# Router logits with the weights stationary in two column halves of the array, in a one-core transformer layer

## The chip, the core and the metric

The kernel runs on one core of a Trainium2 chip. Its engines are TensorE (PE, with its weight loads shown apart as PEld), VectorE (DVE), ScalarE (ACT), GpSimd (POOL) and SyncE (SP), which issues most transfers (SPq is its queue). The metric is the device time of one execution in microseconds (us), less being better; what is compared is the median of several executions.

## What is computed

One layer with 512 tokens and a model width of 1024, all float32: a mixer (gated recurrences), a layer norm, and a mixture of experts with 64 experts of which each token takes 6, beside a shared expert. The change lies in the router at the head of the mixture:

```python
def moe_ffn(h, router_w, router_bias, we_gate, we_up, we_down, ws_gate, ws_up, ws_down):
    xt = h.reshape(B * L, D)                                     # 512 x 1024
    scores = jax.nn.sigmoid((xt @ router_w).astype(jnp.float32)) # 512 x 64
    _, idx = lax.top_k(scores + router_bias, TOP_K)
    s_sel = jnp.take_along_axis(scores, idx, axis=-1)
    wts = s_sel / jnp.sum(s_sel, axis=-1, keepdims=True) * ROUTED_SCALE
    y = routed_experts(xt, idx, wts, we_gate, we_up, we_down) + swiglu(xt, ws_gate, ws_up, ws_down)
```

## The kernel before, in words

The tokens are four tiles of 128 (TT = 4, T = 512); the contraction of 1024 is 8 blocks of 128 (KB = 8); E = 64 experts, P = 128. The first part of the kernel (to about 500 us) is the mixer. `out_and_route` follows, and then `experts`, which works through the expert weights pair by pair from a ring of buffers in on-chip memory, with SP issuing the loads (`load_chunk`, L784) as buffers come free.

Inside `out_and_route` the order of work is written out by hand for each engine; engines meet at semaphores. On PE: `project(2)`, `project(3)` (L170, the output projection of a tile), `turn(t)` (eight transposes of a tile of h1, the normed hidden state, L1033), `logits(t)` (L1039), then `shared_up(0)` (L1046, the shared expert's first product), the counting of the chosen experts (L1083 to L1091), and so on until the tables that say which token goes to which expert's slot. On DVE: `mixed(t)` (L1165 to L1171) and `normed(t)` (L1175 to L1177, whose last step sets `h1_ready`), then the choice of experts, whose first use by PE waits for `chosen_ready` (set by L1207), then the tables; the last of its steps sets `tables_read` (L1280), for which SP waits before it issues further expert weights. On ACT: `root(t)` (L1133, a square root for tile t's norm), `take(t)` (L1137, the copy of a turned tile from PSUM to `h1T`, which sets `h1T_taken`), the sigmoid (L1149). ACT's order is `root(0)`, `root(1)`, `root(2)`, `take(0)`, `take(1)`, `root(3)`, `take(2)`, `take(3)`, sigmoid.

The logits of a tile before the change: the stationary operand is a block of h1T (128 x 128, so 128 columns are loaded), the moving one is the block of the router's weights (128 x 64), and eight products add up in a 64-column strip of bank 0 (R), tokens on partitions. Each float32 product shows as two matmul records and two weight loads in the trace. The column a product writes to in the array follows from where its output starts in PSUM: `gate_up` in `experts` (L1382) writes the two experts of a pair to the two halves of the partitions, with 64-column weights, and `down` (L1423) writes quarters.

Of the kernel before, what the change touches and what calls it, by code (L numbers as in the profile page):

```python
# [18 lines left out]
P = 128  # L19
D = 1024  # L20
KB = D // P
META = 16
T = 512
TA = META + T
TT = T // P
# [12 lines left out]
E = 64  # L38
# [43 lines left out]
ACT = mybir.ActivationFunctionType  # L82
# [29 lines left out]
def program(nc, a, out, stop=9, dbg=None):  # L112
    with ExitStack() as whole:
# [49 lines left out]
        with nc.Block() as block:  # L163
            out_and_route(nc, block, a, sem, sb, banks, pair, mem, top, raw_at, pairs)
            experts(nc, block, a, sem, mem, pairs, out)
# [615 lines left out]
def load_chunk(sp, a, sem, to, name, expert, c):  # L781

    src = a["w_gate_up"][expert, :, c] if c < 2 else a["w_down"][expert]
    return sp.dma_start(to, src).then_inc(sem(name), 16)  # L784


def chunk_at(mem, third, s, c):

    return mem["first"][:, PAIR * c + s] if third == 2 else mem["raw"][:, CHUNKS * (PAIR * third + s) + c]


def raw_here(third, c):

    return f"raw_here_{third}_{c}"
# [109 lines left out]
def out_and_route(nc, block, a, sem, sb, banks, pair, mem, top, raw_at, pairs):  # L904
# [8 lines left out]
    def sb_first(name, shape):  # L913
        at = low[0]
        low[0] += (int(np.prod(shape[1:])) * 4 + 63) // 64 * 64
        assert low[0] <= top[0], name
        return sb(name, shape, at=at)

    h1T = sb_first("h1T", [P, KB, T])
# [3 lines left out]
    rw = sb_first("rw", [P, KB, E])  # L923
# [3 lines left out]
    onehot = sb_first("onehot", [P, ITEMS])  # L927
    count = sb_first("count", [P, EXTRA])
    steps6 = sb_first("steps6", [P, STEPS])
    e_col = sb_first("e_col", [P, 1])  # L930
    tok = sb_first("tok", [P, TT, 2])
    stats = sb_first("stats1", [P, TT, 2, 6])
    mv = sb_first("mv1", [P, TT, 2])
    rs = sb_first("rs1", [P, TT, 2])
# [3 lines left out]
    def sb_late(name, shape):  # L938
        at = late[0]
        late[0] += (int(np.prod(shape[1:])) * 4 + 63) // 64 * 64  # L940
        assert late[0] <= raw_at + RING * CHUNK_W * 4, name
        return sb(name, shape, at=at)
# [3 lines left out]
    sc = sb_late("scores", [P, TT, E])  # L946
# [23 lines left out]
    R, PO, SM = banks[0], banks[1], banks[7]  # L970
# [8 lines left out]
    @block.sync  # L979
    def _(sp):  # L980
        sp.dma_start(g1[:], a["norm_rows"][2:3].broadcast_to([P, D])).then_inc(sem("ln1_here"), 16)
        sp.dma_start(b1[:], a["norm_rows"][3:4].broadcast_to([P, D])).then_inc(sem("ln1_here"), 16)
        for t, n in ((rw, "router_w"), (rbias, "router_bias"), (before, "before"), (before2, "before2"),
                     (count, "count"), (steps6, "steps6"), (e_col, "e_col"), (iota, "iota"),
                     (onehot, "onehot"), (tok, "tok")):
            src = a[n].broadcast_to([P, E]) if n == "router_bias" else a[n]
            sp.dma_start(t[:], src).then_inc(sem("route_here"), 16)
        sp.dma_start(ws_gu[:], a["ws_gate_up"]).then_inc(sem("shared_here"), 16)
        sp.dma_start(ws_dn[:], a["ws_down"]).then_inc(sem("shared_here"), 16)
        sp.dma_start(pairs.tok_row[:], a["tok_row"]).then_inc(sem("tok_row_here"), 16)  # L990

        def bring(third, u, c):
            load_chunk(sp, a, sem, chunk_at(mem, third, u, c), raw_here(third, c), PAIR * third + u, c)

        def ring(slot):
            bring(slot // (CHUNKS * PAIR), slot // CHUNKS % PAIR, slot % CHUNKS)

        for slot in range(NORM_CHUNK):
            if slot not in (MERGED_CHUNK, MERGED_CHUNK + 1):
                ring(slot)  # L1000
        for t in range(TT):
            sp.wait_ge(sem("h1_ready"), t + 1)
            sp.dma_start(h1_rows[t * P:(t + 1) * P], acc[:, t]).then_inc(sem("h1_stored"), 16)

        sp.wait_ge(sem("mix_done"), TT)
        for slot in (MERGED_CHUNK, MERGED_CHUNK + 1, NORM_CHUNK):
            ring(slot)
        sp.wait_ge(sem("tables_read"), 1)
        for slot in range(NORM_CHUNK + 1, RING):
            ring(slot)  # L1010
        sp.wait_ge(sem("shared_up_done"), 4)
        for c in range(2):
            for u in range(PAIR):
                bring(2, u, c)
        bring(2, 1, 2)
        sp.wait_ge(sem("shared_done"), TT)
        bring(2, 0, 2)

    @block.tensor
    def _(pe):  # L1020
# [7 lines left out]
        def turn(t):  # L1028
            pe.wait_ge(sem("h1_ready"), t + 1)
            if t >= 2:  # L1030
                pe.wait_ge(sem("h1T_taken"), t - 1)
            for k in range(KB):
                last = pe.transpose(pair[2 + t % 2][:, k * P:(k + 1) * P], acc[:, t, k::KB], ident[:])  # L1033
            last.then_inc(sem("h1T_done"), 1)

        def logits(t):
            pe.wait_ge(sem("h1T_taken"), t + 1)
            for k in range(KB):
                last = pe.matmul(R[:, t * E:(t + 1) * E], h1T[:, k, t * P:(t + 1) * P], rw[:, k],  # L1039
                                 start=(k == 0), stop=(k == KB - 1))  # L1040
            return last

        def shared_up(i, ks=range(KB)):
            m = gate_first[i]
# [21 lines left out]
            turn(t)  # L1066
        project(3)
        turn(2)
        pe.wait_ge(sem("route_here"), 16 * 10)

        pe.wait_ge(sem("mix_taken"), 3)
        for t in range(TT - 1):
            logits(t)
        turn(TT - 1)
        logits(TT - 1).then_inc(sem("logits_done"), 1)

        pe.wait_ge(sem("shared_here"), 32)
        pe.wait_ge(sem("mix_taken"), TT)
# [2 lines left out]
        for n, of in numbers:  # L1081
            for t in of:
                last = pe.matmul(TOT[:, n * E:(n + 1) * E], ones[:], chosen[:, t, 0], start=(t == of[0]), stop=(t == of[-1]))  # L1083
        for t in range(TT):
            for u in range(t):
                pe.matmul(PO[:, t * E:(t + 1) * E], ones[:], chosen[:, u, 0], start=(u == 0), stop=False)
            last = pe.matmul(PO[:, t * E:(t + 1) * E], before[:], chosen[:, t, 0], start=(t == 0), stop=True)
        last.then_inc(sem("place_done"), 1)
        for n, of in numbers:
            for t in of:  # L1090
                last = pe.matmul(SM[:, n:n + 1], chosen[:, t].rearrange("p a e -> p (a e)"), ones[:, 0:1],  # L1091
                                 start=(t == of[0]), stop=(t == of[-1]))
# [5 lines left out]
        for t in range(TT):  # L1098
            last = pe.transpose(PO[:, t * P:(t + 1) * P], pw[:, t], ident[:])
# [29 lines left out]
    @block.scalar  # L1129
    def _(act):  # L1130
        def root(t):
            act.wait_ge(sem("var1_ready"), t + 1)
            act.activation(rs[:, t, 1:2], rs[:, t, 0:1], ACT.Sqrt).then_inc(sem("std1_ready"), 1)  # L1133

        def take(t):
            act.wait_ge(sem("h1T_done"), t + 1)
            act.activation(h1T[:, :, t * P:(t + 1) * P], pair[2 + t % 2][:, :].rearrange("p (k c) -> p k c", k=KB),  # L1137
                           ACT.Copy).then_inc(sem("h1T_taken"), 1)

        for t in range(EARLY):  # L1140
            root(t)
        root(2)
        take(0)
        take(1)
        root(3)
        take(2)
        take(3)
        act.wait_ge(sem("logits_done"), 1)
        act.activation(sc[:].rearrange("p t e -> p (t e)"), R[:, 0:TT * E], ACT.Sigmoid).then_inc(sem("scores_ready"), 1)  # L1149
        act.wait_ge(sem("shared_up_done"), 1)  # L1150
        act.activation(aT[:, 0], banks[2][:, :], ACT.Silu).then_inc(sem("silu_ready"), 1)
        act.wait_ge(sem("pwT_done"), 1)
        act.activation(pwT[:].rearrange("p t c -> p (t c)"), PO[:, :], ACT.Copy).then_inc(sem("pwT_ready"), 1)
        act.wait_ge(sem("shared_up_done"), 3)
        act.activation(aT[:, 1], banks[3][:, :], ACT.Silu).then_inc(sem("silu_ready"), 1)
        pairs.take_x(act, 0)

    @block.vector
    def _(v):
# [26 lines left out]
            mixed(t)  # L1186
            normed(t)

        v.wait_ge(sem("route_here"), 16 * 10)
        v.wait_ge(sem("scores_ready"), 1)  # L1190
        st(v.tensor_tensor(bs[:], sc[:], each(rbias[:].rearrange("p (a e) -> p a e", a=1)), ALU.add))
        for t in range(TT):
            st.add(v.max(top8[:, t], bs[:, t]))
# [465 lines left out]
```

## Time and profile before

| | us |
|---|---|
| median of 3 runs | 1176.17 (1171.91 to 1176.63) |
| profiled execution, its own time | 1172.07 |
| its span, first to last instruction | 1170.2 |
| PE busy | 1121.9 (96%) |
| DVE busy | 741.0 (63%) |
| ACT busy | 443.1 (38%) |
| mean granted TensorE clock | 0.993 |

Busy shares are means over stages that have different limits. The profiled execution is one run: its span is 1.9 us shorter than its own time, and it is 4.1 us under the median. Times in the views are counted from the start of the span. A matmul's duration in the trace contains its way through the array, so records that follow one another overlap; what one of a row of them costs is the distance between their starts.

### The profile page before, as it was taken

The numbers are of one execution on the slowest core, as the hardware profiler recorded it, in microseconds if no ns is written. First come the engines' busy times: TensorE is split into PE (matmuls) and PEld (weight loads), VectorE is DVE, ScalarE is ACT, GpSimd is POOL, SyncE is SP. The second block draws the span as 40 slices with busy tenths as digits, with TensorE's granted clock in tenths as the row PEclk, the third lists the DMA queues.
The fourth block names the chain that finished last, engine by engine and source line by source line (L and its number), as shares of the span: only waits on it lengthen the run. The fifth ranks groups of instructions, "written<-read, shape, count | busy, mean of one in ns | idle before, by whom it ended". The sixth has DMA issues, their size and how long they took to land.

```text
span 1170.2 us, 18925 instructions
## 1 busy us (share of the span) xinstructions
PE 1121.9 (96%) x6912; PEld 696.0 (59%) x6912; DVE 741.0 (63%) x1268; ACT 443.1 (38%) x692; POOL 210.0 (18%) x116
## 2 busy tenths in 40 slices
PE   5999999999999999999999999999999999999993
PEld 4879888888888888645643444444444444444441
DVE  8868585858585858584554555555555555555557
ACT  6756565656576657401102221112211222211224
POOL 1433333424242424201010000000000000000000
PEclk9999999999999999999999999999999999999997
DMA  6121212121121212229269999999999999999971
GB/s 236 41 109 41 108 44 104 51 97 64 84 74 74 88 60 95 85 93 405 106 250 420 419 421 419 419 419 420 419 419 417 416 413 415 411 418 414 410 300 72
DMA packets 48295, 285.85 MB, mean 244 GB/s; under 512 B 9088, under 2 KB 10624, under 8 KB 16528
## 3 DMA queue, kind: packets, MB, share of 16 engines
q1 hardware_dynamic: 43088, 272.96, 57.5%
q0 software_dynamic: 5184, 12.59, 2.8%
q8 instruction: 14, 0.23, 0.1%
q14 instruction: 9, 0.07, 0.0%
HBM read 287.62 MB, written 4.19 MB: 249 GB/s over the span
## 4 chain that ended last, share of the span: by engine, by line
PE 36%; SPq 13%; DMA 3%; DVE 2%; issue 1%; ACT 1%; DVEq 0%; POOLq 0%
PE pair L1382 14%; SPq L784 12%; PE pair L1423 7%; PE pair L1413 6%; DMA first<-in_w_gate_up 2%; PE pair L170 2%; PE pair L887 2%; PE pair L1046 1%; SPq L1353 1%; DMA xg<-h_rows,idx 1%; PE pair L1039 1%; PE pair L1393 1%; PE pair L854 0%; DVE acc L1571 0%; ACT first L1490 0%
## 5 line engine op out<-in xcount | busy, mean ns | idle before, releaser
L376 PE MATMUL pair<-hT,w_parts 128*128 128x264 f32 (+1 forms) x2112 | 375.9, 337 | 2.0 <-DVE hT L636 1.6
L376 PEld LDWEIGHTS pair<-hT,w_parts 128*128 128x128 f32 x2112 | 319.4, 188 | 48.1 <-issue 4.2
L223 POOL TENSOR_TENSOR w_parts<-w_raw,w_parts 128x1024 fp32r<-128x1024 f32 x66 | 167.4, 2538 | 306.7 <-ACT w_parts L217 295.1
L1513 DVE TENSOR_TENSOR acc<-acc,pair 128x512 f32<-128x512 f32 x280 | 170.6, 681 | 39.3 <-PE pair L1413 39.3
L1382 PE MATMUL pair<-raw,xgT 128*64 128x512 f32 x768 | 170.2, 595 | 0.0
L879 POOL DMA_INDIRECT xg<-h_rows,idx x36 | 35.8, 994 | 530.4 <-DVE idx L873 530.4
L1504 DVE TENSOR_TENSOR act_a<-act_s,pair 128x256 f32<-128x256 f32 x35 | 14.7, 421 | 170.8 <-ACT act_s L1466 170.8
L1473 ACT ACTIVATE y_hi<-pair,small 128x512 fp32r<-128x512 f32 x70 | 48.1, 687 | 196.9 <-PE pair L1423 196.9
L1382 PEld LDWEIGHTS pair<-raw,xgT 128*64 128x64 f32 x768 | 53.2, 137 | 115.9 <-issue 115.9
L1466 ACT ACTIVATE act_s<-pair 128x256 f32<-128x256 f32 x35 | 13.4, 383 | 224.9 <-PE pair L1382 224.9
L1423 PE MATMUL pair<-raw,aT 128*32 128x512 f32 x768 | 87.4, 595 | 0.0
L1413 PE MATMUL pair<-y_hi,ST 64*128 64x512 f32 (+1 forms) x280 | 78.7, 431 | 1.6 <-DVE y_lo L1526 1.6
L1382 PE MATMUL pair<-first,xgT 128*64 128x512 f32 x352 | 78.2, 595 | 0.2 <-DMA first<-in_w_gate_up 0.2
L1526 DVE SCALAR_TENSOR_TENSOR y_lo<-pair,small,y_hi 128x512 fp32r<-128x512 f32 x70 | 52.6, 751 | 36.4 <-ACT y_hi L1473 33.4
L1413 PE MATMUL pair<-y_lo,ST 64*128 64x512 f32 (+1 forms) x280 | 71.2, 391 | 0.0
L217 ACT ACTIVATE w_parts<-w_raw 128x1024 fp32r<-128x1024 f32 x67 | 70.3, 1050 | 0.0
L170 PE MATMUL pair<-w_raw,merged 128*128 128x512 f32 x128 | 55.6, 594 | 1.7 <-DVE acc L1165 1.6
L1382 PEld LDWEIGHTS pair<-first,xgT 128*64 128x64 f32 x352 | 24.4, 137 | 53.5 <-issue 53.5
L887 PEld LDWEIGHTS pair<-ident,xg 128*128 128x128 f32 x288 | 34.9, 194 | 29.9 <-issue 29.9
L703 DVE SCALAR_TENSOR_TENSOR xc<-xr,par,xc 128x528 f32<-128x528 f32 x24 | 51.8, 2157 | 0.6
L1413 PEld LDWEIGHTS pair<-y_hi,ST 64*128 64x128 f32 (+1 forms) x280 | 36.6, 186 | 25.5 <-issue 18.4
L900 ACT ACTIVATE xgT<-pair 128x512 f32<-128x512 f32 x72 | 39.1, 595 | 28.3 <-PE pair L887 28.3
(289 smaller groups left out, 1301.1 us busy)
## 6 DMA issues: line engine op xcount, KB each, us to landing
raw<-in_w_gate_up SPq DMA_DIRECT2D x96, 1024.0 KB
raw<-in_w_down SPq DMA_DIRECT2D x48, 1024.0 KB
first<-in_w_gate_up SPq DMA_DIRECT2D x44, 1024.0 KB
w_raw<-in_w_in SPq DMA_DIRECT2D x36, 1024.0 KB, 6.6
first<-in_w_down SPq DMA_DIRECT2D x22, 1024.0 KB
xin<-in_x SPq DMA_DIRECT2D x4, 512.0 KB, 5.4
ws_gu<-in_ws_gate_up SPq DMA_DIRECT2D x1, 2048.0 KB, 7.7
h_rows<-acc SPq DMA_DIRECT2D x4, 512.0 KB, 21.2
```

The source lines that it names most:

```text
L170: return pe.matmul(banks[2 * (t % 2) + n][:, :], mem["merged"][:, j, t * P:(t + 1) * P], mem["w_raw"][:, j // 2, j % 2, n * 512:(n + 1) * ...
L217: act.activation(w[:, n % PARTS, 0], w_raw[:, n // 2, n % 2], ACT.Copy).then_inc(sem("w_hi_ready"), 1)
L223: pool.tensor_tensor(w[:, n % PARTS, 1], w_raw[:, n // 2, n % 2], w[:, n % PARTS, 0].bitcast(F32), ALU.subtract).then_inc(sem("w_lo_ready" ...
L376: last = pe.matmul(o, w[:, n % PARTS, pw, k * P:(k + 1) * P], hT[ph][:, k, of], start=(k == 0 and m == 0), stop=(k == KB - 1 and m == 2))
L703: ins = v.scalar_tensor_tensor(xc[:], xr[:, i:i + TA], c(C_W0 + i), xc[:], ALU.mult, ALU.add)
L784: return sp.dma_start(to, src).then_inc(sem(name), 16)
L887: last = pe.transpose(self.by_item(self.XT[k // 4][:, (k % 4) * P:(k % 4 + 1) * P]), self.xg[b][:, k::KB], self.mem["ident"][:])
L1382: last = pe.matmul(GU[half[s], :], xgT[:, (KB // 2) * c + k, half[s]], w[s][:, k * 2 * F:(k + 1) * 2 * F], start=(c == 0 and k == 0), stop ...
L1413: last = pe.matmul(SUM[g + i], ST[b][of, t * P:(t + 1) * P], part[of, m * 512:(m + 1) * 512], start=(part is y_hi), stop=(part is y_lo))
L1423: last = pe.matmul(Y[m][rows, :], aT[:, j, rows], w[n % PAIR][:, j * D + m * 512:j * D + (m + 1) * 512], start=(j == 0), stop=(j == 1), ti ...
L1513: v.tensor_tensor(part, part, SUM[g], ALU.add).then_inc(sem("sum_free"), 1)
L1526: v.scalar_tensor_tensor(y_lo[:, cols], Y[m], w_now, y_hi[:, cols].bitcast(F32), ALU.mult, ALU.subtract).then_inc(sem("y_ready"), 1)
```

## The change

The router's weights become the stationary operand: a block of 128 x 64 is loaded into one column half of the array, even blocks of the contraction into the left half and odd ones into the right, and h1T moves through with tokens as columns. The logits then stand with experts on partitions, even parts on partitions 0 to 63 and odd parts on 64 to 127. ACT copies them to a new buffer `halves`; four products with `two`, a constant that holds two 64 x 64 identities one above the other, turn them back to tokens on partitions and add the two parts on the way. Tiles 0 to 2 are one group of 384 columns in bank 0 (R), tile 3 a group of 128 columns in bank 1 (PO). The turned-back logits go to PO, from where the sigmoid reads. `two` is one more constant to load (64 columns, 32 KB), ahead of the shared expert's weights on SP's queue, and its semaphore count rises from 10 to 11.

```diff
+    two = sb_first("two", [P, E])
+    halves = sb_first("halves", [P, T])
...
-                     (onehot, "onehot"), (tok, "tok")):
+                     (onehot, "onehot"), (tok, "tok"), (two, "two")):
...
-        def logits(t):
-            pe.wait_ge(sem("h1T_taken"), t + 1)
+        def logits(t, tiles):
+            pe.wait_ge(sem("h1T_taken"), t + tiles)
+            of = slice(t * P, (t + tiles) * P)
+            to = R if t == 0 else PO
             for k in range(KB):
-                last = pe.matmul(R[:, t * E:(t + 1) * E], h1T[:, k, t * P:(t + 1) * P], rw[:, k],
-                                 start=(k == 0), stop=(k == KB - 1))
-            return last
+                half = slice(k % 2 * E, (k % 2 + 1) * E)
+                last = pe.matmul(to[half, of], rw[:, k], h1T[:, k, of], start=(k < 2), stop=(k >= KB - 2),
+                                 tile_position=(0, k % 2 * E))
+            last.then_inc(sem("logits_done"), 1)
...
-        pe.wait_ge(sem("route_here"), 16 * 10)
+        pe.wait_ge(sem("route_here"), 16 * 11)
         pe.wait_ge(sem("mix_taken"), 3)
-        for t in range(TT - 1):
-            logits(t)
+        logits(0, TT - 1)
         turn(TT - 1)
-        logits(TT - 1).then_inc(sem("logits_done"), 1)
+        logits(TT - 1, 1)
+        pe.wait_ge(sem("scores_ready"), 2)
+        for t in range(TT):
+            last = pe.matmul(PO[:, t * E:(t + 1) * E], halves[:, t * P:(t + 1) * P], two[:], start=True, stop=True)
+        last.then_inc(sem("logits_done"), 1)
...
-        act.wait_ge(sem("logits_done"), 1)
-        act.activation(sc[:].rearrange("p t e -> p (t e)"), R[:, 0:TT * E], ACT.Sigmoid).then_inc(sem("scores_ready"), 1)
+        for n, of in enumerate((slice(0, T - P), slice(T - P, T))):
+            act.wait_ge(sem("logits_done"), n + 1)
+            act.activation(halves[:, of], (R, PO)[n][:, of], ACT.Copy).then_inc(sem("scores_ready"), 1)
+        act.wait_ge(sem("logits_done"), 3)
+        act.activation(sc[:].rearrange("p t e -> p (t e)"), PO[:, 0:TT * E], ACT.Sigmoid).then_inc(sem("scores_ready"), 1)
...
-        v.wait_ge(sem("route_here"), 16 * 10)
-        v.wait_ge(sem("scores_ready"), 1)
+        v.wait_ge(sem("route_here"), 16 * 11)
+        v.wait_ge(sem("scores_ready"), 3)
```

## Rows read from the trace of the kernel before

**Rows 1.** The page: GB/s in 40 slices of the span; the chain's shares by engine.
```profile
GB/s 236 41 109 41 108 44 104 51 97 64 84 74 74 88 60 95 85 93 405 106 250 420 419 421 419 419 419 420 419 419 417 416 413 415 411 418 414 410 300 72
...
PE 36%; SPq 13%; DMA 3%; DVE 2%; issue 1%; ACT 1%; DVEq 0%; POOLq 0%
```

**Rows 2.** The chain that ended last, in order of time: start, us, what.
```profile
548.06 5.32 PE pair L1039 x48
553.38 1.10 PE pair L1033 x8
...
555.58 2.00 PE pair L1039 x16
...
911.99 3.62 PE pair L1423 x32
...
1075.04 28.76 DMA first<-in_w_gate_up
```

**Rows 3.** The timeline, 547 to 565 us: start, us, engine, line, operation [idle before].
```profile
547.01 1.05 PE L1033 MATMUL pair<-ident,acc 128*128 128x128 f32 x8
...
550.22 0.20 ACT L1133 ACTIVATE rs<-rs 128x1 f32<-128x1 f32 x1 [13.46 <-DVE rs L1171]
550.33 1.00 ACT L1137 ACTIVATE h1T<-pair 128x1024 f32<-128x1024 f32 x1
...
551.97 1.28 DVE L1177 SCALAR_TENSOR_TENSOR acc<-acc,rs,b 128x1024 f32<-128x1024 f32 x1
...
554.50 1.02 ACT L1137 ACTIVATE h1T<-pair 128x1024 f32<-128x1024 f32 x1 [3.17 <-PE pair L1033]
555.55 1.28 ACT L1149 ACT_TABLE_LOAD   x1
...
557.42 7.08 PE L1046 MATMUL pair<-h1T,ws_gu 128*128 128x512 f32 x16
...
557.62 0.38 ACT L1149 ACTIVATE scores<-pair 128x256 f32<-128x256 f32 x1 [0.79 <-PE pair L1039]
...
563.03 0.29 DVE L1207 COPY chosen<-chosen 128x256 f32<-128x256 f32 x1
...
564.34 1.22 PE L1083 MATMUL pair<-chosen,ones 128*128 128x64 f32 x10
```

**Rows 4.** The timeline of PE in `experts`, where column halves are used.
```profile
1103.94 3.65 PE L1382 MATMUL pair<-first,xgT 128*64 128x512 f32 x16 [0.24 <-DMA first<-in_w_gate_up]
...
1123.06 1.16 PE L887 MATMUL pair<-ident,xg 128*128 128x128 f32 x8
```

**Rows 5.** The timeline of SP's queue: a load before the ring's, and one behind `tables_read`.
```profile
522.23 0.43 SPq L988 DMA_DIRECT2D ws_gu<-in_ws_gate_up  x1
...
595.33 0.33 SPq L784 DMA_DIRECT2D raw<-in_w_gate_up  x1
```

**Rows 6.** Stretches: us, busy of PE PEld DVE ACT POOL, granted clock, DMA share, GB/s.
```profile
565.00:576.00 11.00, 11.00 (x56) 7.17 (x55) 6.47 (x25) 0.14 (x1) 0.00 (x0) 1.00 0.00 0
...
1154.20:1154.40 0.20, 0.00 (x0) 0.00 (x0) 0.00 (x0) 0.17 (x2) 0.00 (x0) 0.61 0.00 0
```

**Rows 7.** Groups by line: shape, count | busy us, mean ns of one | idle before.
```profile
L1039 PEld LDWEIGHTS pair<-rw,h1T 128*128 128x128 f32 x64 | 7.3, 192 | 1.3 <-ACT h1T L1137 1.3
L1382 PEld LDWEIGHTS pair<-raw,xgT 128*64 128x64 f32 x768 | 53.2, 137 | 115.9 <-issue 115.9
L900 ACT ACTIVATE xgT<-pair 128x512 f32<-128x512 f32 x72 | 39.1, 595 | 28.3 <-PE pair L887 28.3
```

**Rows 8.** The timeline of PE: its longest standstill inside the kernel; its last records.
```profile
42.57 0.66 PE L392 MATMUL pair<-ident,vT 128*128 128x128 f32 x4 [1.93 <-ACT vT L522]
...
1151.08 0.61 PE L1413 MATMUL pair<-y_lo,ST 128*128 128x512 f32 x2
```

**Rows 9.** Transposes of one form, 10 to 17 and 500 to 560 us: ns min/median/max.
```profile
L347 PE MATMUL pair<-ident,acc x22: 421/421/478, 11.1 to 16.9; 128*128 128x128 f32 x22
...
L1033 PE MATMUL pair<-ident,acc x32: 272/273/375, 531.5 to 554.2; 128*128 128x128 f32 x32
```

## The prediction

> **What bounds the kernel now.** I read the page first: its slices, then the shares of its chain [rows 1]. From the 22nd slice (614 us) to the 38th the DMA engines move 410 to 421 GB/s without a pause; before them only one slice comes near that. The chain spends 36% of the span on TensorE (PE) and 13% on SyncE's queue (SPq), which waits to issue expert weights. Next came the chain in order of time [rows 2]: up to 912 us it runs on PE, then along SPq, with one weight transfer of 28.76 us close to its end. So the expert stage is a stream of weights that starts when the routing tables have been read (SPq's load at 595.33 [rows 5]; the DMA share is still 0.00 in 565 to 576 [rows 6]) and then runs full to the end. What delays the tables delays that stream, and with it the end, one for one. The router lies on this path, since nothing runs beside it that could take its place. So I price the change by how much later PE begins `shared_up(0)`, the first work after the logits. It begins at 557.42 [rows 3].
>
> **The stretch before, step by step.** PE finishes the transposes of tile 2 at 548.06, spends 5.32 us on the logits of tiles 0 to 2 (48 records, two for each of 24 products, so 0.111 each), then turns tile 3 (1.10), ACT copies it (1.02), and the logits of tile 3 take 2.00 (16 records) [rows 2, 3]. The eye must go to what the first group is waiting beside. VectorE finishes h1 of tile 3 at 551.97 + 1.28 = 553.25 [rows 3], and PE's logits end at 553.38: PE is only just as late as VectorE. ScalarE copies tile 2 at 550.33 to 551.33, late, since `root(3)` (550.22) stands ahead of `take(2)` in its order [rows 3]. The old code covered that: `logits(0)` and `logits(1)`, 32 records by 0.111 = 3.6 us, filled 548.06 to 551.6.
>
> **What the change does to tiles 0 to 2.** One product now covers three tiles, so its wait asks for `h1T_taken` 3 at once. PE stands still from 548.06 to 551.33 + 0.06 = 551.39 (0.06 is the step from ACT's end to PE, 554.50 + 1.02 to 555.58). That is 3.33 us of idleness that was not there. Then come 8 products, 16 records, of 384 columns, alternating between the array's halves. The nearest rows have exactly this form with 512 columns: `gate_up`'s 16 records take 3.65 us from a standstill [rows 4], so 384 columns take 3.65 x 0.75 = 2.74. PE is done at 554.13, and eight transposes after such a group take 1.16 in the timeline with their tail [rows 4], as against 1.05 at 547.01 in full-array mode [rows 3]; on the chain I count 1.10. ACT's copy of tile 3 can start at about 555.25 where it started at 554.50: **+0.75**. Bounds: with no tail at all (0.14 of the 3.65, which leaves 0.219 a record and 0.165 for 384 columns) 2.6, so +0.6; if the halves did not overlap, 0.43 a record as in `shared_up(0)`, 16 in 7.08 [rows 3], times 0.75, so 5.2 in all and +3.2. The 32 records fewer bring nothing, since the group ends on VectorE and ACT either way. The saving in PE's work (5.32 to 2.74) lies inside the new standstill.
>
> The Trainium skill, "TensorEngine Tiling (Array Packing)", section "Key Properties", says that a change of tiling mode drains TensorE; by that rule the transposes behind the group start later. The row pair agrees in sign, 1.16 against 1.05, so by the rule the sum would be some 0.1 higher, and by the chain's 1.10 as it stands.
>
> **Tile 3.** 16 records of 128 columns with a 64-column weight. Before, the records were spaced by the weight load of 128 columns (0.192 each, at 0.111 apart). A 64-column load takes 0.137 [rows 7], and the difference, 0.055 for 64 columns, says that the spacing halves as well, to 0.058. The products stream as long as that (384 columns were 0.165 apart, so 128 are 0.055). No row shows it, so the bounds are 0.058 and the old 0.111: 15 x 0.058 + 0.3 (tail) = 1.17 us, or 2.0. I take 1.17, because both the load and the stream of the nearest rows shrink with columns.
>
> **The turn back, all of it new and in line.** ACT's first copy (384 columns) follows `take(3)` and ends before the logits of tile 3, so it is hidden by them; were it not, it costs 0.5. The second (128 columns) starts 0.04 after PE and takes 0.29 (0.59 for 512 columns [rows 7], 0.38 for 256 [rows 3], so 0.09 per 128 and some 0.2 fixed). PE starts 0.06 later: 4 products of the old logits' form, 8 records by 0.111 = 0.89, before `shared_up(0)` can follow. From the start of tile 3's logits to the start of `shared_up(0)`: 1.17 + 0.04 + 0.29 + 0.06 + 0.89 = 2.45, against 557.42 - 555.58 = 1.84 before: **+0.61** (+1.46 with the upper bound of 2.0). Queued behind the new wait on PE is everything to the tables: `shared_up`, the counts, `pw`.
>
> The sigmoid's table load (1.28, at 555.55) was hidden under the last logits [rows 3]. ACT now reaches it only after the second copy, so the sigmoid starts 0.29 + 1.30 after the logits; that puts `chosen_ready` some 0.15 later than the PE sum. It was there at 563.32 and PE used it at 564.34 [rows 3], so 1.0 us of cover hides it; with the cover gone it would cost 0.15.
>
> **The rest.** The load of `two` is one more issue on SPq ahead of the shared weights, the ring's first seven loads and the stores of h1: 0.43 + 0.04 us each later [rows 5]. All of these have landed long before the pause of DMA at 565 to 576 [rows 6], so nothing. The `route_here` count of 11 is reached well before 548. The new buffers stand where the stage has room. VectorE's wait on 3 instead of 1 is the same event.
>
> **The clock.** At the end of the kernel PE's last record is done at 1151.08 + 0.61 = 1151.69, and the granted clock falls from 1.00 to 0.5 inside 1154.20 to 1154.40 [rows 6, 8], some 2.55 us later. The longest standstill inside the kernel after which it stayed up is 1.93 us [rows 8]. The new one is 3.33 us, with a few transposes ahead of it. I expect a fall. The Trainium skill's "TensorE: Matmul & The Clock Gate", section "HAM oscillation — how this bites in real kernels", warns of just this, and the end of this trace bears it out. What a record costs at the lower level (1.2 GHz) stands in the first transposes: 421 ns in place of 273, and twice the spacing [rows 9] (the clock column has no event there, the durations show it). If it falls as the group begins and comes back at its end, the price is up to 2.7, and none if it stays up; if it stayed low up to `shared_up(0)`, 2.74 + 0.9 + 0.96 + 0.89 = 5.5. I take **+1.7**: those first transposes reached full speed while they still ran, so the clock comes back under work, and part of the group should run fast.
>
> **Sum.** 0.75 + 0.61 + 1.7 = +3.1 us. The profiled execution took 1172.07 (span 1170.2, 1.9 around it), so 1175.2 by its own time. It was among the quickest shown; the median of the runs is 1176.17, and the same sum on it gives 1179.3. I put 1179.
>
> **The rivals.**
> - *The clock stays up.* For it: 3.33 us is not far from 1.93, and no fall inside the kernel is on record. Then +1.4: 1177.5.
> - *The halves don't run side by side,* because two records of one half follow each other. Against it: `gate_up` has the same order and overlaps. +3.2 + 1.46 = +4.7: 1180.9, the clock aside.
> - *Slower by more than the measurement can tell.* The clock falls and stays low through the transposes, tile 3's logits and the turn back, as the first transposes ran at 421 ns from 11.1 to 16.9, for 6 us [rows 9]: 1.4 + 5.5 = +6.9, 1183. It decides from 4.5 us of lost clock, which needs it low over 9 us of PE's time.
> - *The end doesn't move*, as the delay is made up in the DMA-bound stage. Against it: the stream begins behind the tables. 0: 1176.2.
> - *Faster.* It would need the first group to have been the bound; VectorE's 553.25 speaks against it.
>
> **Chances.** Clock falls for part of the stretch, as forecast: 0.50. Clock stays up: 0.27. No overlap: 0.05. Low throughout: 0.10. End unmoved: 0.06. Faster: 0.02. A measurement of this kernel can tell about 0.5%, 5.9 us; the runs shown spread over 4.7. Slower by that is the low clock, half of the no-overlap case, and a little of the spread: 0.13; faster 0.03; within it 0.84. The range takes the spread of the runs with the cases: from 1173 (the quickest run with +1.4) to 1183 (the low clock on the median).
>
> **What would show it.** PE idle from 548 to 551.4, released by ACT's copy of tile 2. 16 records over about 2.7 us at full clock, 5 at half. The tile 3 logits about 0.06 apart. Then a copy of 0.29, a table load behind it, 8 records before `shared_up(0)` begins at 558.8 (clock up) to 560.5. SPq's load behind the tables moves from 595.33 by the same amount, and the span with it. The prediction is wrong if `shared_up(0)` moves and that load or the end does not, if the idle stretch is missing, or if the clock is low far beyond the first group.

## The result, and the profile after

The changed kernel is slightly slower: a median of 1178.86 us (1175.51 to 1182.41, 18 executions) against 1176.04 (1171.91 to 1180.54, 18 executions), ratio 1.0026 with a 95% interval of 1.0014 to 1.0037. The forecast was 1179, from a sum of +3.1 us on a median of 1176.17; measured is +2.8.

The profiled execution has a span of 1175.3 us, 5.1 more than the one before. The timeline around the router, as in [rows 3] (start, us, engine, line, operation):

```profile
548.92 1.04 PE L1035 MATMUL pair<-ident,acc 128*128 128x128 f32 x8
549.12 1.22 DVE L1179 SCALAR_TENSOR_TENSOR acc<-acc,pair 128x1024 f32<-128x1024 f32 x1 [9.47 <-PE pair L170]
...
552.24 1.00 ACT L1148 ACTIVATE h1T<-pair 128x1024 f32<-128x1024 f32 x1
...
553.39 4.50 PE L1046 MATMUL pair<-h1T,rw 128*64 128x384 f32 x16 [3.42 <-ACT h1T L1148]
553.88 1.28 DVE L1191 SCALAR_TENSOR_TENSOR acc<-acc,rs,b 128x1024 f32<-128x1024 f32 x1
...
557.82 1.16 PE L1035 MATMUL pair<-ident,acc 128*128 128x128 f32 x8
559.01 1.02 ACT L1148 ACTIVATE h1T<-pair 128x1024 f32<-128x1024 f32 x1 [5.76 <-PE pair L1035]
559.93 0.48 ACT L1161 ACTIVATE halves<-pair 128x384 f32<-128x384 f32 x1
560.09 1.09 PE L1046 MATMUL pair<-h1T,rw 128*64 128x128 f32 x16 [1.11 <-ACT h1T L1148]
561.23 0.28 ACT L1161 ACTIVATE halves<-pair 128x128 f32<-128x128 f32 x1 [0.81 <-PE pair L1046]
561.52 1.28 ACT L1163 ACT_TABLE_LOAD   x1
...
561.56 1.10 PE L1085 MATMUL pair<-two,halves 128*128 128x64 f32 x8 [0.38 <-ACT halves L1161]
562.50 4.08 PE L1053 MATMUL pair<-h1T,ws_gu 128*128 128x512 f32 x9
562.81 0.38 ACT L1163 ACTIVATE scores<-pair 128x256 f32<-128x256 f32 x1
...
600.22 0.14 DVE L1294 CAST plan<-q 1x1 int32<-1x1 f32 x1
```

Three lines of the same view of the kernel before, to set beside it:

```profile
547.21 1.22 DVE L1165 SCALAR_TENSOR_TENSOR acc<-acc,pair 128x1024 f32<-128x1024 f32 x1 [9.44 <-PE pair L170]
...
553.31 1.16 PE L1033 MATMUL pair<-ident,acc 128*128 128x128 f32 x8
...
595.16 0.14 DVE L1280 CAST plan<-q 1x1 int32<-1x1 f32 x1
```

Count the times from the start of `mixed(3)` on VectorE (549.12; 547.21 before), called the reference point below; it follows the end of `project(3)` on PE by 0.04 us. What lies ahead of it has a variance of its own. PE stands still for 3.42 us, released by ACT's copy of tile 2. The group of three tiles then takes 4.50 us and ends 2.7 us after VectorE's h1 of tile 3 (553.88 + 1.28 = 555.16), the transposes follow, and from the start of tile 3's logits (560.09) to `shared_up(0)` (562.50) it takes 2.41 us, 1.84 before. `shared_up(0)` begins 13.38 us after the reference point, 10.21 before: +3.17. The tables are read at 600.22 (the step that sets `tables_read`), 51.10 us after it, 47.95 before: +3.15. From there to the end of the span it is 575.1 us in both.

The granted clock, in stretches (us, then busy of PE, PEld, DVE, ACT, POOL, then clock, DMA share, GB/s), shows why a group that takes 2.80 us elsewhere (e1 and e2 below) took 4.50; its second half lists a stretch in the mixer, 80 us earlier:

```profile
554.00:554.20 0.20, 0.20 (x4) 0.14 (x2) 0.20 (x1) 0.00 (x0) 0.00 (x0) 1.00 1.04 430
554.20:554.40 0.20, 0.20 (x4) 0.03 (x1) 0.20 (x1) 0.00 (x0) 0.00 (x0) 0.64 0.94 389
554.40:557.60 3.20, 3.20 (x12) 1.20 (x8) 0.77 (x1) 0.00 (x0) 0.00 (x0) 0.50 1.00 364
557.60:557.80 0.20, 0.20 (x2) 0.00 (x0) 0.00 (x0) 0.00 (x0) 0.00 (x0) 0.82 1.61 389
...
472.00:474.00 2.00, 2.00 (x16) 1.77 (x15) 0.33 (x1) 1.99 (x3) 0.00 (x0) 0.58 0.53 137
474.00:476.00 2.00, 2.00 (x6) 1.55 (x6) 1.64 (x5) 1.73 (x2) 0.00 (x0) 0.56 1.01 326
```

The clock falls to its lower level (0.50, 1.2 GHz) some 0.9 us after the group has begun, and is back 3.4 us later, while the group still runs. The second stretch explains most of the other 1.9 us of the span, by which the reference point stands at 549.12 and not at 547.21: in this execution the clock also fell at 472, behind 64 short records of the mixer (16 columns each), where the change touches nothing. Those records begin 0.36 us later than before the change (469.41 against 469.05), and the other 1.5 us arise behind them. So the span's +5.1 is not the change's; the time from the reference point, +3.1, is.

### The profile page after: what moved, and what is told of

The parts are those of the page before. It is cut to its first block, busy times and chain, and to the rows that moved or that the text cites. A ratio compares the mean times of both kernels' runs of the same rounds, so it can differ in the third digit from the quotient of the medians.

```text
span 1175.3 us, 18880 instructions
## 1 busy us (share of the span) xinstructions
PE 1125.7 (96%) x6888; PEld 695.7 (59%) x6888; DVE 738.6 (63%) x1268; ACT 443.8 (38%) x694; POOL 209.8 (18%) x116
## 4 chain that ended last, share of the span: by engine, by line
PE 38%; SPq 10%; DMA 3%; DVE 2%; issue 1%; ACT 1%; DVEq 0%; POOLq 0%
PE pair L1396 15%; SPq L784 9%; PE pair L1437 8%; PE pair L1427 7%; DMA first<-in_w_gate_up 2%; PE pair L887 2%; PE pair L170 2%; PE pair L1053 1%; DMA xg<-h_rows,idx 1%; SPq L1367 1%; PE pair L1407 1%; PE pair L854 1%; PE pair L1046 0%; DVE acc L1585 0%; ACT first L1504 0%
```

## The experiments

All are compared with the kernel before, run on the same chip. The ratios are those on record and not quotients of the two medians, so the two can differ by up to 0.2%. The experiments ran on four chips; where one is set against the changed kernel's 1178.86, two series are compared. The edits of the first four are short; each is on the changed kernel unless it says otherwise.

**e1: ScalarE's order.** Tile 2's copy goes ahead of the square root of tile 3.

```diff
-        root(3)
         take(2)
+        root(3)
         take(3)
```

> The changed kernel with one exchange on ScalarE: take(2) stands ahead of root(3). Theory A (the first group is late because its wait for tile 2's copy makes PE stand still, and the standstill lowers the clock): PE stands still 1.1 us in place of 3.4, the group of 384 columns starts about 1.2 us after the transposes of tile 2 and takes 2.75 us at full clock, it ends before VectorE has h1 of tile 3, and the transposes of tile 3 start where they did before the change. From the end of project(3) to the start of shared_up(0): 10.8 us, as against 13.4 in the changed kernel and 10.2 before; the time is before +0.6 (ratio to before 1.0005). Rival B (the column halves themselves bring the slow record spacing, 0.29 us, and the clock goes with them): the group still takes 4.5 us, ends after VectorE, and about half of the loss stays: 12.5 us, before +2.

Measured: 1176.49 against 1175.30, ratio 1.0014 (0.9991 to 1.0036). Its timeline of PE, and then one stretch with its clock (0.50, third from the end of the row):

```profile
551.59 2.80 PE L1046 MATMUL pair<-h1T,rw 128*64 128x384 f32 x16 [1.20 <-ACT h1T L1148]
...
555.64 1.16 PE L1035 MATMUL pair<-ident,acc 128*128 128x128 f32 x8 [1.25 <-DVE acc L1191]
...
557.91 1.72 PE L1046 MATMUL pair<-h1T,rw 128*64 128x128 f32 x16 [1.11 <-ACT h1T L1148]
...
560.00 1.97 PE L1085 MATMUL pair<-two,halves 128*128 128x64 f32 x8 [0.37 <-ACT halves L1161]
```

```profile
558.60:565.00 6.40, 6.03 (x22) 3.84 (x19) 2.34 (x9) 3.23 (x4) 0.00 (x0) 0.50 0.99 394
```

The schedule part of theory A holds: the group starts early, takes 2.80 and not 4.5 (which ends rival B), and the transposes wait for VectorE (1.25 us) and start 6.10 us after the reference point (549.54), just where they did before the change (553.31 - 547.21). The clock part was too simple. With no gap over 1.25 us, the clock fell at 558.3 and stayed low for 6.8 us: the turn back took 1.97 in place of 1.10, and `shared_up(0)` 8.6 in place of 6.9. So `shared_up(0)` began 12.22 us after the reference point, where 10.8 was expected, and in this one execution the tables come 51.60 us after it, no better than in the changed kernel. The median of its 12 executions is 2.4 us under the changed kernel's 1178.86, where 2.5 was expected, but the spread is wide (1172.61 to 1184.87) and the intervals of the two ratios overlap (0.9991 to 1.0036, 1.0014 to 1.0037): the times don't show the gain by themselves.

**e2: the standstill filled with work that nobody reads.**

```diff
+        pe.wait_ge(sem("h1T_taken"), 2)
+        for t, ks in ((0, KB), (1, KB - 2)):
+            for k in range(ks):
+                pe.matmul(PO[:, t * E:(t + 1) * E], h1T[:, k, t * P:(t + 1) * P], rw[:, k],
+                          start=(k == 0), stop=(k == ks - 1))
         logits(0, TT - 1)
```

> The changed kernel with 28 extra matmul records (14 products of the old logits' form into a bank that is written anew later, their results unused) in PE's standstill; the order of waits is the same. Theory A: the granted clock stays at 1.00, the group of 384 columns still starts with the copy of tile 2 but takes 2.75 us in place of 4.5, and the time is 1.7 us under the changed kernel (before +1.3, stretch from project(3) to shared_up(0) 11.6 us). Rival B (clock falls because of the group's own form, not of the standstill): the group stays at 4.5 us and nothing is gained.

Measured: 1177.07, ratio 1.0018 (1.0005 to 1.0032). PE's timeline:

```profile
555.57 3.24 PE L1082 MATMUL pair<-rw,h1T 128*128 128x64 f32 x28
...
559.06 2.80 PE L1046 MATMUL pair<-h1T,rw 128*64 128x384 f32 x16 [0.26 <-ACT h1T L1153]
...
561.79 1.16 PE L1035 MATMUL pair<-ident,acc 128*128 128x128 f32 x8
...
566.48 7.08 PE L1053 MATMUL pair<-h1T,ws_gu 128*128 128x512 f32 x16
...
577.79 5.38 PE L1053 MATMUL pair<-h1T,ws_gu 128*128 128x512 f32 x8
```

This takes the clock apart from the schedule. The group still waits for the copy, takes 2.80 us, and `shared_up(0)` starts 11.59 us after the reference point (554.89): +1.38, against +3.17 with the low clock. 4.50 - 2.80 = 1.70 us is the clock's part, +1.38 the schedule's, and the remaining 0.09 us is PE's start behind the copy (0.15 us after ACT's end in the changed kernel, 0.06 here). The median is 1.8 us under the changed kernel's, 1.7 expected, though the intervals of the ratios overlap here too. The clock says it more plainly: 4 of the 13 executions have a mean clock of 0.992 or more, none of the changed kernel's 30. The traced execution is the slowest of the 13. It has a fall of its own further on (578 to 581, at `shared_up(1)`, behind 40 short records of counting) and five stretches of low clock in the mixer, between 18 and 309 us, none of which the edit touches.

**e3: the standstill on the old router.** One wait for `h1T_taken` 3 ahead of the old `logits(0)`.

> The kernel before with one wait added: its logits of tile 0 also wait for the copy of tile 2, as the new group does. All else is the old router. Theory A: PE stands still 3.4 us, the 48 records then take 5.3 us if the clock stays up and up to 7 if it falls as in the changed kernel, and end 3.4 to 5 us after VectorE is done; shared_up(0) starts 3.4 to 5.2 us later than before, and the time is before +3.4 to +5.2. Rival B (the clock falls only with column halves): exactly +3.4, with the clock at 1.00 throughout.

Measured: 1186.0 (4 executions), ratio 1.0089 (1.0066 to 1.0112): +10.7 us, double the upper end expected. PE's timeline:

```profile
554.14 8.90 PE L1039 MATMUL pair<-rw,h1T 128*128 128x64 f32 x48 [3.53 <-ACT h1T L1138]
...
565.85 3.67 PE L1039 MATMUL pair<-rw,h1T 128*128 128x64 f32 x16 [1.11 <-ACT h1T L1138]
```

The clock falls at about 555.9, as theory A wants and with no column half in sight, but comes back only at 573.0: 17.1 us in all at the lower level. The 48 short records take 8.90 us in place of 5.48, the 16 take 3.67 in place of 2.00. The wide group of the changed kernel had the clock back after 3.4 us; this sparse form ran into `shared_up(0)` at half speed.

**e4: the first group cut in two** (tiles 0 and 1, then tile 2), ScalarE's order as changed.

> The changed kernel with the first group cut in two: tiles 0 and 1 (256 columns, ready early), then tile 2 (128 columns). ScalarE's order is as in the changed kernel. Theory A: 256 columns take about 1.9 us and start at once after the transposes, so PE stands still for only about 1.4 us until tile 2's copy is there; tile 2's 16 records take 1.1 us and end before VectorE is done; clock stays up; 10.8 us from project(3) to shared_up(0), time before +0.6. Rival C (each group of column-half records pays a drain at its two ends that the large group hides): some 0.3 us more.

Measured: 1181.68, ratio 1.0056 (1.0037 to 1.0074): a miss, +6.4 us where +0.6 was expected. PE's timeline:

```profile
550.49 1.95 PE L1046 MATMUL pair<-h1T,rw 128*64 128x256 f32 x16
...
553.89 1.09 PE L1046 MATMUL pair<-h1T,rw 128*64 128x128 f32 x16 [1.46 <-ACT h1T L1150]
...
555.82 1.97 PE L1035 MATMUL pair<-ident,acc 128*128 128x128 f32 x8 [0.83 <-DVE acc L1193]
```

Every record is where theory A put it until 555.8: 1.95 and 1.09 us (rival C's extra 0.3 is not there), transposes released by VectorE. Then the clock goes, and stays low for 10.2 us and, later, 3.4 more (behind the counting); the tables come 54.18 us after the reference point (549.72). All six executions have a mean clock of 0.987 or less. Small groups with pauses of 0.8 to 1.5 us between them cost more here than one wide group behind a pause of 3.4.

**e5: the change for tiles 0 to 2, with PE's gaps filled.** ScalarE's order as in e1; blocks of `shared_up(0)` on the columns of tiles 0 to 2 fill the waits; tile 3 keeps the old form. The order on PE:

```python
        logits(0, TT - 1)
        ...                                       # two waits
        shared_part(0, range(0, 2), early)        # columns of tiles 0 to 2
        turn(TT - 1)
        pe.wait_ge(sem("scores_ready"), 1)        # tiles 0 to 2 copied to halves
        for t in range(TT - 1):
            pe.matmul(PO[:, t * E:(t + 1) * E], halves[:, t * P:(t + 1) * P], two[:], start=True, stop=True)
        shared_part(0, range(2, 3), early)
        logits_of_last(TT - 1)                    # the old form, straight to PO
        shared_part(0, range(3, KB), early)
        shared_part(0, range(KB), late).then_inc(sem("shared_up_done"), 1)
        shared_up(1, range(0, 2))
        pe.wait_ge(sem("chosen_ready"), 1)
```

> The router of the change for tiles 0 to 2 only, with PE's gaps filled: take(2) ahead of root(3); the group of three tiles; then the first two blocks of shared_up(0) on 384 columns until tile 3 can be turned; during ScalarE's copy of tile 3 the turn back of tiles 0 to 2 and one more block of shared_up(0); tile 3's logits in the old form straight into bank 1, so that neither its copy nor its turn back is waited for; two blocks of shared_up(1) moved ahead of the wait for the chosen experts. If the work PE saves in the group (5.3 to 2.8 us) is worth what the chain then lets through, and if gaps of PE are what lowers the clock: the read of the tables stands some 2.5 us nearer to the end of project(3) than before (45.4 in place of 48.0 us), the clock stays at 1.00 through the router, and the time is 2.5 us under before (ratio 0.998), more where before loses to low clock. Rival (VectorE's chain from the sigmoid to the tables is the bound, so filling PE does nothing): the distance stays 48 us.

Measured: 1174.44 against 1174.78, ratio 0.9986 (0.9967 to 1.0005), which does not tell it from the kernel before. Its reference point and the read of its tables:

```profile
551.12 1.22 DVE L1194 SCALAR_TENSOR_TENSOR acc<-acc,pair 128x1024 f32<-128x1024 f32 x1 [9.48 <-PE pair L170]
...
597.20 0.14 DVE L1309 CAST plan<-q 1x1 int32<-1x1 f32 x1
```

The tables are read 46.08 us after the reference point, 1.9 us nearer than before; 2.5 were expected. The clock stays at 1.00 from 520 to 640.

**e6: the same filling on the old router,** as a control.

```diff
         turn(TT - 1)
-        logits(TT - 1).then_inc(sem("logits_done"), 1)
...
-        shared_up(0)
+        shared_part(0, range(0, 2), early)
+        logits(TT - 1).then_inc(sem("logits_done"), 1)
+        shared_part(0, range(2, KB), early)
+        shared_part(0, range(KB), late).then_inc(sem("shared_up_done"), 1)
+        shared_up(1, range(0, 1))
         pe.wait_ge(sem("chosen_ready"), 1)
```

> The same filling on the old router, as a control: two blocks of shared_up(0) during ScalarE's copy of tile 3, one block of shared_up(1) ahead of the wait for the chosen experts; the logits are as before the change. The gap of 1.1 us goes, the group of 5.3 us stays: the read of the tables 0.9 to 1.2 us nearer to project(3) than before, 1 us under before. The difference to e5_filled is what the column halves are worth by themselves, about 1.5 us. Rival: both gain the same, and the column halves are worth nothing even with PE's gaps filled.

Measured: 1175.33 against 1174.78, ratio 0.9985 (0.9965 to 1.0005): the median lies above the one before and the ratio below 1, so the times show no difference. The same two lines:

```profile
553.82 1.22 DVE L1175 SCALAR_TENSOR_TENSOR acc<-acc,pair 128x1024 f32<-128x1024 f32 x1 [9.44 <-PE pair L170]
...
600.55 0.14 DVE L1290 CAST plan<-q 1x1 int32<-1x1 f32 x1
```

Tables 46.73 us after the reference point: 1.2 nearer than before, the upper end of what was expected. So the traces put what the column halves add, once the gaps are filled, at 0.65 us and not 1.5. The two differ in more than the halves (e5 also has ScalarE's new order and moves one block more of each product), so this is the worth of e5's router as a whole, from one trace of each. Most of what is gained is the filling.

**e7: both kinds of blocks in one column half,** on e1. All eight products go to partitions 0 to 63.

> The kernel of e1_take_first with all eight blocks of the contraction in one column half (no second half, so nothing is added in the turn back, which reads 64 partitions). It measures whether the halves run side by side. If they do: the group of three tiles takes 16 x 0.32 = 5.1 us in place of 2.8 and ends about 1.1 us after VectorE's h1 of tile 3, tile 3's records are 0.11 apart and not 0.06: +0.9 us; the time is e1_take_first +2, clock aside. If they don't, both take the same time.

Measured: 1178.94, ratio 1.0022 (0.9999 to 1.0046). PE's timeline, to be read against e1's 2.80 and the changed kernel's 1.09:

```profile
552.94 5.34 PE L1045 MATMUL pair<-h1T,rw 128*64 128x384 f32 x16 [1.21 <-ACT h1T L1147]
...
560.48 1.96 PE L1045 MATMUL pair<-h1T,rw 128*64 128x128 f32 x16 [1.11 <-ACT h1T L1147]
```

The halves do run side by side: 5.34 against 2.80 for 384 columns, 1.96 against 1.09 for 128. The clock stayed up through the router in this execution, with the same gaps as e1. The tables come 50.72 us after the reference point (550.89), +2.8: 1.2 since the transposes start so much later, 0.9 for tile 3, and the rest for the turn back.

**e8: the kernel before, unchanged.**

> The kernel before, unchanged, as if it were a change: what this comparison shows between equals (ratio within 0.2% of 1), and a second trace of it. In the profiled executions so far the time rises by 0.3 to 0.4 us with each us of low granted clock. If the clock falls in some executions of the kernel before too, as its mean clock of 0.986 to 0.993 says, this trace may show at which gap; if it falls only behind the kernel's end, the trace shows no fall before 1150 us and the spread has another source.

Measured: 1173.74 against 1174.78, ratio 0.9984 (0.9961 to 1.0007). Between equals the comparison shows 0.16%; a single ratio such as e5's or e6's, at 0.14 and 0.15%, proves nothing by itself. The trace repeats the distances to 0.01 us: `shared_up(0)` at 10.22, the tables at 47.94 after the reference point. It has no fall before 1150 us either.

**e10: the changed kernel, unchanged.**

> The changed kernel, unchanged, for a second trace and more executions. If PE's standstill of 3.4 us and the sparse work behind it lower the clock in every execution: this trace too has a fall between the end of the transposes of tile 2 and shared_up(0), and no execution has a mean clock above 0.990 (of the 18 measured none had, of 60 of the kernel before 22 had 0.992 or more). If the fall in the first trace was chance, some executions reach 0.992, and this trace may show shared_up(0) 11.7 us behind project(3) in place of 13.4.

Measured: 1179.74 against 1175.34, ratio 1.0029 (1.0009 to 1.0049). PE's timeline:

```profile
555.31 4.46 PE L1046 MATMUL pair<-h1T,rw 128*64 128x384 f32 x16 [3.42 <-ACT h1T L1148]
```

The fall is there again, 3.4 us long and at the same place, and `shared_up(0)` is at 13.34 after the reference point (551.04). Of its 12 executions two have a mean clock of 0.991, against the expectation of none above 0.990, and none has 0.992.

**e11: more of the filling.**

> e5_filled with two things more (e9_filled_more mended: the second column strip of the first two blocks joins the open accumulation and does not start one of its own). Two blocks of shared_up(0) on tiles 0 and 1 fill the 1.2 us in which PE waits for the copy of tile 2. Tile 3's logits use the column halves too (1.1 in place of 2.0 us), the copy of its 128 columns goes to VectorE, which is idle then, so that ScalarE's table load stays hidden, and one more block of shared_up(0) covers that copy; its turn back is 2 records. If PE's total work and gaps between project(3) and the tables are what the path consists of: tables read 44.6 us after the end of project(3) (before 47.95, e5 46.08), and the time 3.3 us under before at equal clock, ratio 0.997. Rival (VectorE's chain behind the sigmoid is the bound by now): no nearer than e5's 46.1.

(The earlier writing that this text names, e9, has no result: it began an accumulation anew while one was open.) Measured: 1172.71 against 1174.95, ratio 0.9983 (0.9967 to 0.9999), where 0.997 was expected. It has the lowest median of the study, 6 us below the changed kernel's; but its 0.17% is no more than the 0.16% that e8 shows between equals, so that it is faster than the kernel before is not shown by the times. The tables come at 594.17, 45.76 after the reference point (548.41), not 44.6: a miss. Its timeline shows what stopped it:

```profile
564.63 0.29 DVE L1245 COPY chosen<-chosen 128x256 f32<-128x256 f32 x1
...
564.98 1.33 PE L1117 MATMUL pair<-chosen,ones 128*128 128x64 f32 x10 [0.24 <-DVE chosen L1245]
```

PE now waits for VectorE's choice of experts, which it had been 1 us behind in [rows 3]. Up to that point the rival of the expectation holds: VectorE's chain has become the bound. The choice is ready 16.51 us after the reference point, later than e5's 16.12, since the sigmoid that it starts from begins at 10.88 and not 10.41: the blocks put ahead of tile 3's turn back delay it. More filling there would, by this, bring nothing; no run tries it.

**The clock over all executions.** Each execution's mean granted clock is on record. Those of the kernel before at 0.993 correspond to some 16 us at half clock, which is what lies behind PE's last work ([rows 6]); 0.991 or less is a fall inside the kernel. At 0.992 there can be one: the traced execution of e11 has 0.992 and a low stretch of 3.4 us from 18 us on.

| kernel | executions | with mean clock 0.992 or more | median of those, us | median of the rest, us |
|---|---|---|---|---|
| before (its executions beside the experiments) | 94 | 30 | 1173.23 | 1176.25 |
| changed (both series) | 30 | 0 | | 1179.1 |
| e5_filled | 12 | 2 | 1171.46 | 1174.70 |
| e11_filled_more | 12 | 6 | 1171.77 | 1173.25 |

A straight line through the 94 executions of the kernel before (time against the low time that the mean clock gives, 2 x (1 - clock) x span) rises by 0.37 us for each us at half clock. The same line through the 18 of the changed kernel rises by 0.33, and carried on to the 16.4 us of an execution without a fall it stands at 1174.8, against 1172.9: +1.9 us, near the +1.38 of the schedule alone. That is an estimate from outside the data, since no execution of the changed kernel has less than 21 us.

## Why the prediction was right

- **What bounds the kernel.** Right. In every trace of the study the end follows the read of the tables by 574.8 to 575.4 us, whether the tables came 45.8 or 59.1 us after the reference point. The delay is carried to the end one for one; the rival of an unmoved end is out.
- **The group behind the standstill.** Right in mechanism and size: 3.33 us of idleness worked out, 3.42 found; 2.74 us for the group at full clock, 2.80 found in e1 and e2. (The 0.09 us is the start behind the copy, told under e2.) The copy of tile 3 should start 0.75 us later without the clock; in e2 it starts 8.10 after the reference point, 7.29 before: +0.81.
- **The halves side by side.** Right, shown by e7. (The bound of that rival for tile 3, 2.0 - 1.17 + 0.61, is +1.44 and not +1.46; nothing hangs on it.)
- **Tile 3 and the turn back.** Worked out 2.45 us, found 2.41, the spacing of 0.058 included (16 records in 1.09 us). The second copy took 0.28 (0.29). The sigmoid followed its table load, as forecast, and cost nothing: `chosen_ready` is set at 568.53, and PE uses it at 569.42. The drain of the Trainium skill's "TensorEngine Tiling (Array Packing)", section "Key Properties", is not singled out by any run. The prediction read 1.16 us for transposes behind such a group, against 1.05 in full-array mode, as agreeing with it in sign. That reading does not hold: the transposes of tile 3 took 1.16 us in the kernel before as well (553.31, the line above), behind full-array logits, and again in e1, behind a pause of 1.25.
- **The clock.** The fall was forecast at half the chance, its price at 1.7 us; both traces of the changed kernel show it, at 1.70 and 1.66, and none of its 30 executions has a mean clock above 0.991. The price was a choice between 0 and 2.7, not a result; that it came out to the hundredth is luck, and the clock fell not as the group began but 0.9 us later. The reason given, one long standstill, is only a part. e3 shows that the standstill alone brings the fall with the old router too, e2 that filling it takes the fall away at that place. But e1 and e4 fell with no pause over 1.5 us, and e7, with the pauses of e1, did not fall there. The Trainium skill's "TensorE: Matmul & The Clock Gate", section "HAM oscillation — how this bites in real kernels", tells of long waits between bursts; here a row of pauses of 0.8 to 1.5 us with short records between them was enough in some executions. Nor is 1.93 us a length after which the clock stays up, as the prediction took it from one trace: the same standstill of 1.9 to 2.0 us in the mixer is followed by a fall that begins at 43.7 to 45.4 us in seven of the twelve traces (e2 to e7, e10).
- **The rival "slower by more than can be told"** needed the clock low for over 9 us of PE's time. The changed kernel doesn't reach it, but e3 (17.1 us) and e4 (13.6 us) do, so it deserved its tenth.
- **The size of the sum.** +3.1 forecast, +3.15 between the traces' reference points and tables, +2.8 between the medians. The interval of the ratio is +1.6 to +4.4 us, so the 0.3 us between the two need no cause. The +1.4 of the rival with the clock up lies only just outside it; what rules that rival out is the traces.

What stays open: which of the short pauses lower the clock in a given execution. The same kernel falls in one and not in another (e1's 12 executions range from 0.982 to 0.993, and one has 0.992 or more, against 7 of the 25 of the kernel before beside it), and one trace of each kernel can't say more.

## What to carry to other kernels

When per-tile work is merged into one wider call, the wait becomes that of its last tile: ask what the engine did meanwhile, and what stands ahead of that tile's producer in its own order. The saving in PE's work (5.3 to 2.8 us) was real and bought nothing, since the group had ended together with another engine's work; it shortened the way to the tables (by 1.9 us in e5 and 2.2 in e11, of which the filling gives 1.2 without it, e6) only when other ready work was moved into the time it freed. On PE a pause can be priced twice, once by its length and once by the half clock behind it, and the second price differed with what followed: 3.4 us at half clock behind the wide group, 17.1 behind the narrow records of e3.

## What was not expected of the hardware

- The clock falls inside the kernel in most executions of the kernel before (64 of 94 by their mean clock). Neither of its two traces has such a fall, so where they lie is not shown; in the other traces there are falls in the mixer, which no edit touches, at 44, 126, 300, 416 and 472 us among others. The spread of its times goes with them: 0.37 us for each us at half clock, with a correlation of 0.88.
- After a pause of 3.5 us, 48 records of 64 columns and what followed ran 17.1 us at half clock (e3), while 16 records of 384 columns in two column halves had the full clock back after 3.4 us.
- Weight loads of 64 columns into alternating halves let records of 128 columns follow each other at about 0.06 us (16 in 1.09), where all in one half gave 0.11 (16 in 1.96).
